# Recurrence of a three-layer fp32 model: next pair's key panel moved behind the inverse, key norm begun at the walk's end, output in a buffer of its own, gate one pair later

## What is computed

```python
rkv = rkv + (_token_shift(rkv) - rkv) * mu_rkv          # r, k, v: each token mixed with the one before
decay = exp(-exp(w_log)); a = sigmoid(a0 + (xa @ a1) @ a2)
g = sigmoid(xg @ g1) @ g2                               # the gate
kk = k * k_k; kk = kk / max(norm(kk), 1e-12)            # the key norm, per head and token
k = k * (1 + (a - 1) * k_a)
# per head:  S_t = S_{t-1} diag(w_t) + (S_{t-1} (-kk_t)) (kk_t * a_t)^T + v_t k_t^T ;  o_t = S_t r_t
o = (o - mean(o)) * rsqrt(var(o) + GN_EPS) * ln_g + ln_b
o = o + sum(r * k * r_k) * v                            # the bonus
return o * g
```

## Time and profile before

| | |
|---|---|
| median of 3 runs | 2742.94 us (2742.7 to 2747.05) |
| the profiled execution | 2744.07 us, span of its records 2742.2 us |
| busy share of the span | PE 93%, PEld 76%, DVE 51%, POOL 42%, ACT 33% |
| granted TensorE clock, mean | 0.978 |
| panel matmuls (L1800 to L1802) | 3 x 2656, 3154.8 us of records that overlap each other |
| 64x64 products (L2244) | 5632, 205.7 us |
| the recurrence | from about 1500 us to 2019 us of the span |

### The profile page before, as it was taken

The page is one execution under the profiler, slowest core; times in us unless marked ns, Lnnn a source line. Parts: engine busy times, 40 slices in busy tenths (PEclk is TensorE's granted clock), DMA queues, the critical chain, the costliest instruction groups (busy, mean ns, idle before and its releaser), DMA issues.

```text
span 2742.2 us, 46926 instructions
## 1 busy us (share of the span) xinstructions
PE 2553.0 (93%) x18466; PEld 2077.3 (76%) x18466; DVE 1395.3 (51%) x1997; ACT 910.6 (33%) x1444; POOL 1147.4 (42%) x657
## 2 busy tenths in 40 slices
PE   6798899999899998999996999999999988999998
PEld 4575688887787877888875888887887766788886
DVE  3624873345513258454277566666659963321122
ACT  3233422223523334222254333333333334332231
POOL 3433544444444435444454333333333325444442
PEclk8999999999999999999998999999999999999999
DMA  5310223232221112323322111111112222233331
GB/s 152 80 54 16 85 92 100 92 100 85 77 93 35 58 62 85 99 92 94 98 71 73 41 33 41 41 33 33 33 57 87 89 62 83 87 99 98 94 100 54
DMA packets 56465, 202.67 MB, mean 74 GB/s; under 512 B 6768, under 2 KB 7448, under 8 KB 56304
## 3 DMA queue, kind: packets, MB, share of 16 engines
q1 hardware_dynamic: 54144, 195.84, 22.5%
q0 software_dynamic: 1328, 3.68, 0.8%
q10 hardware_dynamic: 832, 0.82, 0.1%
HBM read 196.64 MB, written 3.67 MB: 73 GB/s over the span
## 4 chain that ended last, share of the span: by engine, by line
PE 78%; DVE 11%; issue 4%; ACT 4%; POOL 2%; DMA 0%; DVEq 0%; SPq 0%; ACTq 0%; POOLq 0%
PE banks L1800 21%; PE banks L1801 21%; PE banks L1802 21%; PE banks L2244 8%; ACT sb_pa L635 1%; PE banks L2285 1%; DVE banks L1592 1%; PE banks L2018 1%; DVE sb_zr L1502 1%; POOL sb_pa L1678 1%; PE banks L1980 1%; DVE sb_x L1078 1%; PE banks L2144 1%; PE banks L1933 1%; PE banks L2001 1%
## 5 line engine op out<-in xcount | busy, mean ns | idle before, releaser
L1652 POOL TENSOR_TENSOR sb_wl<-sb_raw,sb_wh 128x1024 fp32r<-128x1024 f32 x365 | 897.3, 2460 | 1235.9 <-ACT sb_wh L454 1235.7
L1800 PE MATMUL banks<-sb_bh,sb_wh 128*128 128x512 f32 x2656 | 1061.8, 400 | 93.9 <-POOL sb_bl L1664 28.0
L1801 PE MATMUL banks<-sb_bl,sb_wh 128*128 128x512 f32 x2656 | 1047.1, 394 | 0.0
L1802 PE MATMUL banks<-sb_bh,sb_wl 128*128 128x512 f32 x2656 | 1045.9, 394 | 0.0
L1800 PEld LDWEIGHTS banks<-sb_bh,sb_wh 128*128 128x128 f32 x2656 | 505.4, 190 | 227.4 <-issue 53.9
L1802 PEld LDWEIGHTS banks<-sb_bh,sb_wl 128*128 128x128 f32 x2656 | 505.1, 190 | 110.5
L1801 PEld LDWEIGHTS banks<-sb_bl,sb_wh 128*128 128x128 f32 x2656 | 505.8, 190 | 107.4 <-issue 2.2
L454 ACT CAST sb_wh<-sb_raw 128x1024 fp32r<-128x1024 f32 x365 | 381.4, 1046 | 542.6 <-PE banks L1802 538.0
L2244 PE MATMUL banks<-sb_m 64*64 64x64 f32 (+1 forms) x5632 | 205.7, 228 | 8.4 <-DVE sb_m L1542 7.6
L2244 PEld LDWEIGHTS banks<-sb_m 64*64 64x64 f32 x5632 | 195.7, 134 | 20.1 <-issue 12.4
L998 DVE SCALAR_TENSOR_TENSOR sb_x<-sb_x,banks 128x512 f32 x72 | 49.5, 688 | 315.0 <-PE banks L1802 315.0
(11 more groups left out here) (319 smaller groups left out, 2628.0 us busy)
## 6 DMA issues: line engine op xcount, KB each, us to landing
sb_raw<-w SPq DMA_DIRECT2D x365, 512.0 KB, 3.5
sb_x<-xT SPq DMA_DIRECT2D x4, 512.0 KB, 6.6
out<-sb_x SPq DMA_DIRECT2D x4, 512.0 KB, 2.7
bias_rows<-sb_brow POOLq DMA_DIRECT2D x1, 1536.0 KB, 35.1
sb_bias<-bias_rows POOLq DMA_DIRECT2D x1, 1024.0 KB, 6.7
sb_pj<-pT POOLq DMA_DIRECT2D x2, 512.0 KB, 3.9
sb_wm<-wm ACTq DMA_DIRECT2D x1, 288.0 KB, 3.4
sb_rope<-rope ACTq DMA_DIRECT2D x1, 256.0 KB, 3.0
```

Of the source, the lines that this page charges most:

```text
L1652: nc.gpsimd.tensor_tensor(wl[:, s, :], raw[:, s, :], wh[:, s, :].bitcast(F32), ALU.subtract).then_inc(lo_ready, 1)
L1800: nc.tensor.matmul(out, hi_a, hi_b, start=first, stop=False)
L1801: nc.tensor.matmul(out, hi_a, lo_b, start=False, stop=False)
L1802: return nc.tensor.matmul(out, lo_a, hi_b, start=False, stop=last)
```

## The change

- *Order of panels.* k comes ahead of the lora panel in pairs 1 to 7. The lora panel of pair c carries the gate factor of pair c-1; one more panel at the end carries the gate factor of pair 7. A lora panel's casts (ACT, POOL) cover 256 columns.
- *Key panel.* PE makes the k panel of pair n+1 in one piece in `half(n)`, between the inverse and `tt`. DVE mixes it at once (`mix_keys`), behind the rates and ahead of `mp`.
- *Mix.* Instead of an ACT copy and two DVE operations from SBUF, DVE reads the panel's PSUM bank: one column, then the whole times 1-mu into a scratch tile, then the shifted bank times mu plus the scratch.
- *Key norm.* In the walk ACT squares the next pair's keys, runs one tiny square root (which brings the sqrt table in), and casts two panels. PE's first work after the walk is `kk`; the key spread follows the mean. On DVE the norm comes ahead of the output's steps.
- *Output.* It has its own buffer (`ob`, in place of `rn`), its squares have `osq`. DVE's output steps come behind R, K and the first t.
- *Gate.* Pair c-1's gate is made in pair c into bank 6 and read there by DVE; ACT's copy is gone. `kr`, which uses bank 6 next, waits for `out`.
- *v panel.* Three of its eight pieces come ahead of `l`, five behind it, with the output spread between.

```diff
-            gt = sb("gt", [P, T], F32, part)
+            osq = sb("osq", [P, T], F32, part)
...
+        ob = rn
...
             def pair(c):
...
+                    key_square(0)
+                st.wait(pair_dve, c, "kmax")
+                st.did(pair_act, "root", nc.scalar.activation(r8[:, 1, :], r8[:, 0, :], ACT.Sqrt))
+                if c:
+                    centred_square(c - 1)
+                    root_of_output(c - 1)
+                else:
+                    split(Idx(0, p0 + 4))
+                split(Idx(0, p0 + 4 * c + 5), 2 * P if c < NC - 1 else D)
+                if c:
                     high(c - 1)
...
                 half(c)
...
                 move("n", M_N)
                 if not last:
-                    split(Idx(0, p0 + 4 * n + 7))
+                    key_square(n + 1)
+                    nc.scalar.activation(r8[:, 5, 0:1], eps[:, 0:1], ACT.Sqrt)
+                split(Idx(0, p0 + 4 * n + 7))
+                if not last:
+                    split(Idx(0, p0 + 4 * n + 8), D if n < NC - 2 else 2 * P)
                 st.wait(half_pe, n, "o7")
-                st.did(half_act, "o", nc.scalar.copy(zr, psum[:, O_BANK, :]))
+                st.did(half_act, "o", nc.scalar.copy(ob, psum[:, O_BANK, :]))
...
+            def mix(c, i, tile, done, own, dst):
+
+                b = (g0 + tile) % 2
+                dve.wait_ge(panel_done, p0 + 4 * c + done)
+                k = NC * i + c
+                V.tensor_scalar(dst[:, 0:1], psum[:, b, 0:1], mu_own[:, k:k + 1], None, ALU.mult)
+                link(V.tensor_scalar(own, psum[:, b, :], mu_own[:, k:k + 1], None, ALU.mult))
+                V.scalar_tensor_tensor(dst[:, 1:T], psum[:, b, 0:T - 1], pcol("mu_rkv", k), own[:, 1:T], ALU.mult,
+                                       ALU.add).then_inc(bank_free[b], 1)
+                tile_moved(c, tile)
...
                 st.wait(pair_act, c, "root")
                 st.did(pair_dve, "kinverse", V.reciprocal(r8[:, 2, :], r8[:, 1, :]))
                 if c:
-                    output_low(c - 1)
+                    centre(c - 1)
...
-                tile_moved(c, 3)
-                link(shift(0, zr))
+                mix(c, 0, 3, 3, sq[:, 0, :], zr)
                 st.did(half_dve, "r", V.tensor_tensor(m_all[:, M_R, :, :], chunks(zr), decay_upto, ALU.mult))
+                if c:
+                    output_inverse(c - 1)
                 link(V.scalar_tensor_tensor(zk, lw, 1.0, zk, ALU.add, ALU.mult))
                 st.did(half_dve, "k", V.tensor_tensor(m_all[:, M_K, :, :], chunks(zk), chunks(em), ALU.mult))
+                first_t(c)
+                if c:
+                    output_scaled(c - 1)
+                    output_gated(c - 1)
                 st.did(pair_dve, "prod", V.scalar_tensor_tensor(sq[:, 1, :], zr, col("r_k", c), zk, ALU.mult, ALU.mult))
-                tile_moved(c, 4)
-                link(shift(2, zv))
+                mix(c, 2, 4, 4, sq[:, 0, :], zv)
...
                     if b in beside:
                         beside[b](n + 1)
+                if n < NC - 1:
+                    mix_keys(n + 1)
...
                 st.did(half_pool, "bd", nc.gpsimd.tensor_tensor(m_all[:, M_BD, :, :], m_all[:, M_B, :, :], last_decay, ALU.mult))
+                low(Idx(0, p0 + 4 * n + 5), 2 * P if n < NC - 1 else D)
                 st.wait(half_dve, n, "k")
...
+                    key_sums(c)
+                    b = tile_bank(c, 3)
+                    receptance(range(3))
                     mean(c - 1)
-                    gate(c)
-                    dense_part(b, 1, range(2, 5))
+                    key_spread(c)
+                    receptance(range(3, NC - 1))
+                    gate(c - 1)
+                    receptance(range(NC - 1, NC)).then_inc(panel_done, 1)
                     variance(c - 1)
...
-                        if i == 2:
-                            st.wait(pair_act, n, "gate")
+                        if name == "kr" and g == 0 and n:
+                            st.wait(post_dve, n - 1, "out")
...
+                v_bank = tile_bank(n, 4)
+                dense_part(n, v_bank, 3, range(3))
+                if n:
+                    st.wait(post_act, n - 1, "oroot")
                 product("l", [(M_A, M_B)], needs=[by_dve("b")])
+                if n:
+                    output_spread(n - 1)
+                dense_part(n, v_bank, 3, range(3, NC)).then_inc(panel_done, 1)
                 product("lr", [(M_B, (M_A, M_R))], needs=[by_dve("r")])
...
                     last_t, last_x = f"t{b}", f"x{b}"
+                if n < NC - 1:
+                    dense_part(n + 1, tile_bank(n + 1, 2), 0, range(NC)).then_inc(panel_done, 1)
                 product("tt", [(M_X, (M_AT, M_W))], needs=[by_dve(last_x), by_act("ab"), by_act("w")])
```

More of the change, by code:

```diff
@@ L365, in build @@
             pair_pe: ["kk", "kspread", "bonus"],
-            pair_act: ["decay", "square", "root", "gate"],
-            pair_dve: ["sums", "mixed", "kmax", "kinverse", "prod"],
+            pair_act: ["decay", "square", "root"],
+            pair_dve: ["sums", "kmax", "kinverse", "prod"],
             post_pe: ["mean", "var", "ospread"],
@@ L844, in decays, with key_square @@
                 st.did(pair_act, "decay", nc.scalar.activation(em, cu, ACT.Exp, scale=-1.0))
+            def key_square(c):
+                b = tile_bank(c, 2)
+                act.wait_ge(bank_free[b], c * 3 + (g0 + 2) // 2 + 1)
+                st.did(pair_act, "square", nc.scalar.activation(sq[:, 0, :], zk, ACT.Square, scale=pcol("k_k", c)))
             def pair(c):
[L848 to L851, removed]
                 if c == 0:
                     split(Idx(0, p0 + 3))
[L854 to L860, removed]
+                    key_square(0)
                 st.wait(pair_dve, c, "kmax")
@@ L884, in high @@
                 st.wait(post_dve, c, "out")
-                st.did(post_act, "high", nc.scalar.copy(bh[1][:, c, :], zr))
+                st.did(post_act, "high", nc.scalar.copy(bh[1][:, c, :], ob))
             def half(n):
@@ L1493, in output_inverse, with output_scaled, output_gated, first_t @@
                 st.did(post_dve, "oinverse", V.reciprocal(r8[:, 4, :], r8[:, 3, :]))
[L1495 removed]
+            def output_scaled(c):
                 st.wait(post_pe, c, "ospread")
[L1498 removed]
+                link(V.scalar_tensor_tensor(ob, ob, col("lnx_g", c), psum[:, 7, :], ALU.mult, ALU.mult))
+            def output_gated(c):
                 tile_moved(c, 5)
[L1500 to L1502 removed]
+                link(V.scalar_tensor_tensor(ob, ob, col("lnx_b", c), sq[:, 1, :], ALU.add, ALU.add))
+                dve.wait_ge(panel_done, p0 + 4 * c + (6 if c < NC - 1 else 5))
+                st.did(post_dve, "out", V.tensor_tensor(ob, ob, psum[:, 6, :], ALU.mult))
             def output_low(c):
                 st.wait(post_act, c, "high")
[L1506 removed]
+                V.tensor_tensor(bl[1][:, c, :], ob, bh[1][:, c, :].bitcast(F32), ALU.subtract).then_inc(opnd_dve, 1)
+            def first_t(n):
+                for g in range(2):
+                    st.wait(half_pe, n, f"l.{g}")
+                    link(V.tensor_tensor(one(g, M_T), bank(f"l.{g}"), each(wm[:, 2, :]), ALU.mult))
+                    st.did(half_dve, f"t1.{g}", V.tensor_tensor(one(g, M_T), one(g, M_T), each(eye[:, :]), ALU.add))
             def half(n):
@@ L1780, in _ @@
                 pair(c)
-            w.p += 4 * NC
+            w.p += 4 * NC + 1
             panels(4 * NC)
@@ L2197, in mean @@
                 st.wait(half_dve, c, "s8")
-                st.did(post_pe, "mean", nc.tensor.matmul(psum[:, 2, :], o64[:, :], zr, start=True, stop=True))
+                st.did(post_pe, "mean", nc.tensor.matmul(psum[:, 2, :], o64[:, :], ob, start=True, stop=True))
             def variance(c):
                 st.wait(post_act, c, "osquare")
-                st.did(post_pe, "var", by_token(3, sq[:, 0, :]))
+                st.did(post_pe, "var", by_token(3, osq[:, :]))
             def output_spread(c):
                 st.wait(post_dve, c, "oinverse")
-                st.did(post_pe, "ospread", spread(5, r8[:, 4, :]))
+                st.did(post_pe, "ospread", spread(7, r8[:, 4, :]))
             def half(n):
```

167 lines of the change are left out of this document (78 added, 89 removed).

## The result

| | before | after |
|---|---|---|
| median (4 runs each) | 2742.82 us | 2712.91 us (2709.48 to 2715.97) |
| ratio, 95% interval | | 0.9889 (0.9871 to 0.9906), that is 30.4 us less (25.8 to 35.4) |
| the profiled execution | 2744.07 us, span 2742.2 | 2709.48 us, span 2707.7 |
| PE busy share of the span | 93% | 94% |

The forecast was 2714.0 us.

The account below looks back on a forecast made before the run. TensorE was taken as the bound, some 59 us of work and 4.2 us idle per pair. Gains of 13.2, 8.3, 7.6, 0.2 and 0.3 less 0.6 make 29.0 us: 2742.94 to 2713.9, say 2714; range 2711 to 2717, 8 in 10: 2709 to 2723.

Parts of the forecast that it names:

- What bounds: Recurrence: TensorE holds some 59 us of work per 63.3 us pair; only 4.2 us of idle time can be won.
- one cold start fewer: Each pair: five panel pieces start cold against six, up to 1.4 us more gain, left in the range.
- Key norm: Walk's end: norm ready at 1.8 us, ahead of the key spread, removing that wait; gain 8.3 us.
- ACT in the walk: ACT's squares, table load and two casts take 4.3 us and end 0.8 us before the walk does.
- The list of DVE up to `out`: DVE's steps from r to `out` end 17.4 us after the walk without collisions, 19.5 with them.
- rival 1: `kr` waits for `out` 0.3 to 1.3 us in 7 pairs, giving back 2 to 9: 2716 to 2723, chance 0.19.
- (a): Lora casts on ACT and POOL cut to 256 columns: neither is the bound, so worth 0 in itself.
- rival 4: Slower: full casts hold DVE's chain from r to `out`, `kr` waits 10 us; 2780 us, chance 0.04.
- (b): Pair 0: earlier key sums gain 0.3 us; a full cast holding the rates product loses 0.6 (0 to 1.5).
- (c): Tail: gate(7) may delay its output spread by 0.5 us; with gate(0) leaving pair 0 (0.7), gain 0.2.
- output in its own buffer, the first t early: gain 13.2: Before `ab`: the banks of `l` are freed early, so the wait goes in all 8 pairs, 13.2 us.
- Rivals 2 to 4: 2: idle time only moves, 2718 to 2729, 0.07; 3: one idle time stays, 2722 to 2727, 0.04; 4: slower, 0.04.

Follow-up runs that it names:

- The kernels with two and five extra operations: Changed kernel with two, or five, unused VectorE operations added ahead of `out` in each pair: medians 2716.62 and 2738.11 us.
- the norm alone: Kernel before with only the key norm moved ahead of the previous pair's output steps on DVE: ratio 1.0008.
- the first t: Kernel before with only the first t moved ahead of the bonus product and the mix of v on DVE: ratio 0.9976, 6.6 us less.
- all three swaps: Kernel before with key norm ahead of output steps, scan behind the last x addition, and first t ahead of the bonus product: ratio 0.9963.
- With the tail filled: Changed kernel with pair 0's key panel started early and the last pair's end woven into the next stage's first panel: median 2706.95 us.

## Why the prediction held, step by step

- *What bounds.* A pair holds 59.2 us of PE work at the full clock. It was forecast from the earlier trace rows at a period of 59.2 and came out at 59.39. The seven later pairs gained 27.8 us, against 27.45 in the sum (7/8 of 13.2, 8.3 and 7.6). No gain from one cold start fewer (up to 1.4 us in the range) can be seen: PE's busy time per pair is 59.23, not less than 59.14.
- *Key norm.* Asked for at t = 4.0 and ready at 1.8 in the prediction; 4.02 and 1.80 in the trace. The reciprocal took 0.20 us beside a cast, as in the earlier trace rows.
- *ACT in the walk.* 4.3 us, done 0.8 us early; measured 4.13 and 1.0. The activation behind the table load starts 0.02 us after it, so no drain beyond the 1.28 us is seen here either.
- *The list of DVE up to `out`.* Predicted 17.4 to 19.5; measured 18.36. r landed at 9.46 against 9.65 and its mix took 1.67 us against 1.55. The mix was not held by POOL. R took 1.01 and the t additions 1.05 and 0.83 beside POOL work, K's first product 0.64: some collisions, not all. `lr`, `kr` and `ab` were put at 17.9, 19.75 and 22.7; they came at 18.1, 19.9 and 22.8.
- *The risk, rival 1.* The cover was given as 0.25 to 2.3 us and was 1.5. In two profiles out of two the wait was 0.2 us, once, in pair 7, where a full cast stands beside the list; the prediction counted on the short cast in all pairs. The kernels with two and five extra operations show that the risk is real: past 1.5 us the wait opens, and then costs its length and some clock.
- *The mis-sized terms.* (a) "Casts cut to 256 columns, worth 0 in itself": with full casts the cover is gone, `out` is 1.8 us later, and the stretch is 3.6 us longer in the one profile (1.1 of it in waits of `kr`), though the medians can't tell the two kernels apart. The prediction had the mechanism in rival 4 (a full cast holds an operation for 2.1 us, as the earlier trace rows) but put the casts of v and k there, not the lora cast that the change shortens. The short cast is what keeps rival 1 away. (b) Pair 0: 13.2/8 + 0.3 - 0.6 = 1.35 us were expected, 2.7 came. The loss of 0.6 did not happen; the product with the rates (L1478) took 1.12 us, less than the 2.24 it took before. The gate that leaves the pair is the rest, which the prediction had set against the tail. (c) The tail: a loss of 0.5 was expected for the gate there. It took 19.22 us before, and 16.78 and 18.34 in the two profiles of after, but with the clock taken out some 16.4 before and 16.8 after. So the loss is about as expected, and the 2.4 us that the tail seems to win are no part of what was forecast.
- *The attribution.* The total was right, but not for the reason that a sum of three separate idle times suggests. The experiments on the kernel before show that the norm alone wins nothing, the first t half of its wait and all three swaps 10.2 us. The step "output in its own buffer, the first t early: gain 13.2" holds only with the rest of DVE's list rebuilt. The prediction did the count that matters, the list from r to `out` against PE's list, but only for the whole; it could not have priced a part by its own wait.
- *Rivals 2 to 4* did not occur in the changed kernel. ACT had 1.0 us of slack, `mp` waited for nothing, and each named cause was real.

The scatter is worth a sentence: between repeats of the changed kernel the time moves by 6.5 us, so 29.0 against 30.4 us is no difference that these runs can tell.

## What to carry to other kernels

A table of waits names what is late, not what can be won. Before adding idle times up, ask for each what the engine named does between this wait and the next: where two waits stand on one list without slack (norm and R here), a swap moves the first into the second; in these runs only work that left the stretch of the list between the two counted. Before a new wait is added, count both lists to it and measure the cover by loading it; what lay past the cover here was paid in full, and the clock added to it in three waits of eight. A cast cut that "isn't the bound" may be what keeps a shared port free at the narrowest place.

## What the runs showed of the hardware

- *POOL and DVE hold each other.* `kd` took 1.50 us before, where it began at 1721.51, inside DVE's product for the bonus (L1479, two SBUF inputs, 1721.35 to 1722.10), with the shift of v behind. In the changed kernel it takes 1.06 us where it began (1703.23) beside a mask that reads PSUM; the t addition behind that mask (L1524, two SBUF inputs) took 1.05 us there, against 0.43 before (L1528), when `kd` and `dg` had ended. The two full-width operations of DVE's mix from PSUM took 0.73 to 0.75 us each in every pair. The Trainium skill, page "SBUF — State Buffer", section "Who interferes with whom", calls the shared port pair an exclusive lock; these durations agree with it.
- *The clock in the tail differs between executions of one kernel.* The windows view of the changed kernel, behind the output spread of pair 7, in its first profile:

```profile
1988.00:1990.00 2.00, 2.00 (x10) 1.66 (x9) 1.32 (x2) 0.62 (x1) 0.00 (x0) 1.00 0.00 0
```

and of the same kernel in its second profile, where the spread began 1.09 us later:

```profile
1989.00:1991.00 2.00, 2.00 (x6) 1.53 (x5) 1.58 (x3) 0.32 (x1) 0.00 (x0) 0.50 0.00 0
```

Both had the same two waits of 0.68 and 1.51 us just before. One stayed at 2.4 GHz, the other fell to 1.2 GHz and its tail took 18.34 us instead of 16.78. The tail of before took 19.22 us, with the clock at 0.50 from 2014 to 2020. So the 2.4 us of the tail in the profiled gain are the clock and not the change. The Trainium skill, page "TensorE: Matmul & The Clock Gate", section "What's actually happening", says that one and the same kernel can run a different number of its matmuls at the slow level from run to run; it says so of a kernel's start, and these two profiles show the like in its middle. With the tail filled, so that no wait above 1.0 us stands in it, the clock was 1.00 throughout in the one profile there is.
